# A two-block transformer kernel on one core: where the loads of the second feed forward's first two tiles stand in SyncE's queue

## The reference

```python
for l in range(DEPTH):                      # DEPTH = 2, h is 256 x 1024
    h = layer_norm(ALPHA * h + 0.5 * swiglu(h, ffn1_gate[l], ffn1_up[l], ffn1_down[l]), ...)
    ...                                     # token mixer, w_out, layer norm
    h = layer_norm(ALPHA * h + cross_attn(h, mem, ca_q[l], ca_k[l], ca_v[l], ca_o[l]), ...)
    h = layer_norm(ALPHA * h + 0.5 * swiglu(h, ffn2_gate[l], ffn2_up[l], ffn2_down[l]), ...)
# swiglu: (silu(x @ w_gate) * (x @ w_up)) @ w_down, inner width 2816 = 22 tiles of 128
# cross_attn ends with o @ ca_o, a 1024 x 1024 matrix
```

## Time and profile before

| | |
|---|---|
| median of three runs | 3466.71 us (3460.61 to 3467.05) |
| the profiled execution's own time | 3480.58 us |
| its span | 3478.8 us |
| mean granted TensorE clock | 0.985 of full speed |
| PE busy | 3171.2 us, 91% of the span |
| DVE busy | 2116.0 us, 61% |
| ScalarE busy | 936.6 us, 27% |
| GpSimd busy | 1198.1 us, 34% |
| bytes moved by DMA | 1163.11 MB, mean 334 GB/s |

### The profile page before, as it was taken

The page is one execution under the profiler, slowest core; times in us unless marked ns, Lnnn a source line. Parts: engine busy times, 40 slices in busy tenths (PEclk is TensorE's granted clock), DMA queues, the critical chain, the costliest instruction groups (busy, mean ns, idle before and its releaser), DMA issues.

```text
span 3478.8 us, 46441 instructions
## 1 busy us (share of the span) xinstructions
PE 3171.2 (91%) x16237; PEld 2519.7 (72%) x16237; DVE 2116.0 (61%) x4203; ACT 936.6 (27%) x2393; POOL 1198.1 (34%) x1129
## 2 busy tenths in 40 slices
PE   8899999989999999989999898878888889978887
PEld 5598888868878888868867655438877855636777
DVE  6686778655555458655554575676554477487544
ACT  2310022210010012220023354334443354433333
POOL 1003553334425433334410143344441044344332
PEclk9999999999999999999999999999999999999999
DMA  8578988689989977689963899999995399999998
GB/s 332 189 273 306 384 340 291 249 305 341 353 305 383 350 281 265 251 302 351 350 215 115 319 401 419 419 421 408 419 421 221 123 396 411 419 421 419 421 421 364
DMA packets 246943, 1163.11 MB, mean 334 GB/s; under 512 B 27256, under 2 KB 29656, under 8 KB 180720
## 3 DMA queue, kind: packets, MB, share of 16 engines
q0 software_dynamic: 152784, 825.30, 59.1%
q1 hardware_dynamic: 93936, 335.48, 27.1%
q10 hardware_dynamic: 48, 0.05, 0.0%
HBM read 1159.62 MB, written 1.10 MB: 334 GB/s over the span
## 4 chain that ended last, share of the span: by engine, by line
PE 60%; DMA 20%; DVE 6%; ACT 5%; issue 4%; POOL 1%; another core or an unknown queue 0%; SPq 0%; DVEq 0%; ACTq 0%; POOLq 0%
DMA ring<-in_peer_uv,idx 19%; PE ps_b L1040 17%; PE ps_a L1048 8%; PE ps_b L594 7%; PE ps_a L975 6%; PE ps_a L581 5%; PE ps_b L845 4%; PE ps_a L979 3%; ACT arena L1245 3%; PE ps_b L603 2%; DVE arena L2049 1%; ACT L1245 1%; ACT wts L1245 1%; DMA ring<-in_ffn 1%; PE ps_b L645 1%
## 5 line engine op out<-in xcount | busy, mean ns | idle before, releaser
L558 POOL DMA_INDIRECT ring<-in_peer_uv,idx x512 | 552.3, 1079 | 1144.3 <-PE ps_a L975 423.4
L2049 DVE SCALAR_TENSOR_TENSOR arena<-ring,h_tm 128x1024 f32<-128x1024 f32 x512 | 624.9, 1223 | 515.5 <-DMA ring<-in_peer_uv,idx 514.6
L520 POOL DMA_INDIRECT ring<-in_peer_uv,idx_now x512 | 574.1, 1121 | 407.4 <-DVE arena L1967 154.4
L1040 PE MATMUL ps_b<-x_t,ring 128*128 128x256 f32 x2816 | 622.2, 379 | 6.1 <-DMA ring<-in_ffn 3.2
L979 PE MATMUL ps_a<-arena,ring 128*128 128x128 f32 x4096 | 519.9, 283 | 107.8 <-ACT arena L1245 107.7
L1040 PEld LDWEIGHTS ps_b<-x_t,ring 128*128 128x128 f32 x2816 | 534.4, 190 | 81.5 <-DMA ring<-in_ffn 5.5
L979 PEld LDWEIGHTS ps_a<-arena,ring 128*128 128x128 f32 x4096 | 482.8, 195 | 145.9 <-ACT arena L1245 145.2
L975 PE MATMUL ps_a<-ring,arena 128*128 128x512 f32 x1024 | 485.2, 610 | 86.8 <-ACT arena L1245 85.7
L1245 ACT ACTIVATE arena<-ps_b 128x256 f32<-128x256 f32 (+2 forms) x213 | 104.0, 490 | 1324.3 <-PE ps_b L1040 771.2
L975 PEld LDWEIGHTS ps_a<-ring,arena 128*128 128x128 f32 x1024 | 182.2, 191 | 335.0 <-ACT arena L1245 175.6
L1048 PE MATMUL ps_a<-arena,ring 128*128 128x256 f32 x1408 | 318.7, 379 | 0.0
(11 more groups left out here) (273 smaller groups left out, 3201.1 us busy)
## 6 DMA issues: line engine op xcount, KB each, us to landing
ring<-in_ffn SPq DMA_DIRECT2D x264, 512.0 KB
wring<-in_second_w SPq DMA_DIRECT2D x232, 512.0 KB
wring<-in_mix_w SPq DMA_DIRECT2D x128, 512.0 KB
ring<-in_ada_rows POOLq DMA_DIRECT2D x36, 512.0 KB, 5.0
ring<-in_peer_uv,idx_now POOLq DMA_INDIRECT x512
ring<-in_peer_uv,idx POOLq DMA_INDIRECT x512
ring<-in_second_w SPq DMA_DIRECT2D x4, 512.0 KB, 15.4
ring<-in_c_rows POOLq DMA_DIRECT2D x1, 1024.0 KB, 7.3
```

The source lines that it names most:

```text
L520: G.indirect_dma_start(rows[:, s, :], None, table, bass.IndirectOffsetOnAxis(ap=idx_now[:, half, s:s + 1], axis=0)).then_inc(rows_in[s], p ...
L558: G.indirect_dma_start(pairs[:, slot, :, :].rearrange("p c d -> p (c d)"), None, a["peer_uv"], bass.IndirectOffsetOnAxis(ap=idx[:, b, s:s ...
L1040: ins = mm(bank[:, part * T:(part + 1) * T], fw[:, ft % 2, part, k * P:(k + 1) * P], x_t[:, k, :], start=k == 0, stop=k == KT - 1)
L2049: V.scalar_tensor_tensor(products[n % 2], pairs[:, at % PAIRS, 0, :], 1.0, h_tm[:, n // SLOTS, :], ALU.mult, ALU.mult, accum_out=dots[:, n ...
```

## The change

For the second feed forward (`w == 1`) of both layers, the call that loads the last four chunks of `mix_w` moves from behind the six loads of the first two tiles to ahead of them. Nothing else differs, and no other engine's program does.

```diff
                 for w in range(2):
+                    if w == 1:
+                        chunk_loads(a["mix_w"], mix_at + (MIX_CHUNKS - WR), WR)
                     for ft in range(2):
                         for part in range(3):
                             ff_loads(l * (2 * FT) + (w * FT + ft), ft, part)
                     if w == 0:
                         mod_row_loads(row_at)
                     else:
-                        chunk_loads(a["mix_w"], mix_at + (MIX_CHUNKS - WR), WR)
                         mod_row_loads(row_at + 1)
                         mod_row_loads(row_at + 2)
```

## The result

The changed kernel takes 3475.45 us (median of 19 runs, 3469.62 to 3484.81); the kernel before, beside it, 3466.02 us (19 runs, 3459.71 to 3471.03). The ratio is 1.0031, 95% interval 1.0023 to 1.0038: slower by 10.7 us (8.0 to 13.2); the medians alone are 9.4 us apart. I had forecast no change at 3466.7, with 3458 to 3474 as the range.

What follows compares the result with a forecast made beforehand. The prediction took PE, busy 3171.2 of 3478.8 us, to set the pace, with no load late on this stretch. All terms were 0, giving 3466.7 us from the runs' median, range 3458 to 3474.

Steps and rivals of the forecast that it cites:

- no change: Whole kernel: time stays at 3466.7 us, chance 0.75; about 0.2%, 7 us, taken as what a measurement can tell.
- What is taken away: Stretch from 709 to 727 us: 3.15 MB of loads leave it, the gathers and DVE don't move; gain 0.
- The output's second half: Its four chunk loads wait for PE's consumption at 746.27 and later, not for the six loads; gain 0.
- The six loads themselves: Issued from 756.85, landed by 767.2, first needed at 783.21: 16 us of cover; cost 0.
- No gathers are in the way: Six loads in their new place: POOL's last gather is issued at 745.04, so q1 runs at its own speed.
- The chunk behind the six: Modulation row's first chunk, queued behind the six: lands at 768.5, wanted at 770.18, 1.7 us to spare; cost 0.
- the second rival: Modulation row's first chunk lands after 770.18 and PE waits in each layer: up to +8.8 us, 3475.5 us; chance 0.12.
- The first rival: PE's idle time ahead of the output, behind ACT's late copy, goes with the loads: up to 10.8 us, 3456 us; chance 0.13.
- The sum against the profiled execution: Whole kernel: 0 against the profiled 3480.58 us, 13.9 us above the runs' median; change of 0 applied to 3466.71 us.
- A margin of 1.7 us: Modulation row's first chunk: time between its forecast landing and PE's need of it, in each layer.

Runs made afterwards that it cites:

- e8: Changed kernel with the modulation row's four chunk loads put ahead of the six loads, against the kernel before (3465.30 us chip): ratio 1.0007.
- e6: Changed kernel with MIX_SUMS 16, 16, 8 instead of 8, 16, 16 (fewer gathers in the stretch), against the kernel before: ratio 1.0041.
- e3: The change in the first layer only, against the kernel before (3491.43 us chip): ratio 0.9994.
- e10: Changed kernel with 16 matmuls of zeros ahead of the output's products in both layers, against the kernel before: ratio 1.0036.
- e2: Changed kernel with the modulation row's four chunk loads put ahead of the six loads, against the kernel before (3491.43 us chip): ratio 0.9988.
- e5: Kernel before with MIX_SUMS 16, 16, 8 instead of 8, 16, 16, old load order, against the kernel before: ratio 1.0052.
- e1: The kernel before again, no edit, against the kernel before (3491.43 us chip): ratio 0.9997.
- e12: The change in the first layer only, against the kernel before (3465.56 us chip): ratio 1.0018.

## Why the prediction was wrong

**What is taken away: right.** The 3.15 MB in the stretch to 727 us delayed nothing. e8 takes them away without the new wait and gains nothing.

**The output's second half: right.** L582 runs 27.89 us without a wait in the changed kernel.

**The six loads themselves: right.** The first gate product never waits for `ffn`, even in e8, where they go out 13.8 us later against the output's start than in the changed kernel.

**"No gathers are in the way": wrong, and this is the step that failed.** It rested on the time at which SP could issue: 756.85, worked out from the earlier trace rows. That time held PE's late start of the output (6.26 us) in it. POOL doesn't follow PE here, since DVE's sums, not the output, free its places. So when the stall (5.1 us) and the low clock behind it (2.1 us) are absent, and the values' products end 1.4 us earlier besides, SP's loads move up by 8.5 us and the gathers stay: last issue at 744.96 in the changed kernel, 745.04 in the earlier trace rows. An issue isn't a landing, either: in the trace of before, the queues from 746 to 750 us show

```profile
q0 software_dynamic: 421, 1.54, 99.4%
```

and 0.26 MB more from 750 to 754. At the forecast's 756.85 that was over. At 748.34 it wasn't: from 748 us on the changed kernel's gathers still move 1.6 MB, 1.6 MB / 0.41 = 3.9 us of all engines, in front of or between the six. They also hold up the four chunk loads ahead of the six, which by 748 us had moved only 1.04 of their 2.10 MB. The sum put right, an estimate with the forecast's own terms: 1.06 + 1.63 + 3.15 + 0.52 = 6.36 MB from 748.0 at 410 GB/s are 15.5 us, with its 1.8 us of latency 765.3; the profile has 765.89, and PE wants the chunk at 761.75. Without the 1.63 MB the same sum gives 761.3. That is just in time, as in e6. With PE late (e3, e10) there is room for the gathers.

**The chunk behind the six: right as a mechanism, wrong in its chance and its price.** This was the second rival, at 0.12 and +8.8 us. Its price came from an old burst's time per MB and was near by luck; the clock term of 1.4 us per layer wasn't in it. Nor do 7 us pass for no change here: with 19 runs a side the interval is 2.6 us to either side. The ring order that I cited from the Trainium skill, "DMA: Bandwidth & Descriptors", section "Queues, rings and completion order", is borne out: the chunk issued at 751.42 landed at 765.89, behind the six loads, the last of which landed at 764.61.

**The first rival: fell.** The late copy does go in the changed kernel's profile, as the rival said it would, but e2 and e3 have it with the loads moved, and e5 is without it with the loads in the old place. It goes with the chip: late in both layers of all three usable profiles where the kernel before takes 3491 us, in time in both layers of all eight experiments where it takes 3465 to 3466. The first profile of before is the one exception: it has the late copy (5.1 and 5.7 us), though the three plain runs beside it take 3461 to 3467 us, and on which chip it ran isn't known.

**The sum against the profiled execution.** I noted 13.9 us between that execution and the median and carried on. The stall ahead of the output and the low clock behind it are 5.1 + 2.1 us in the first layer and 5.6 + 3.0 in the second, 15.8 together: enough for the whole difference. The same holds on the chip of 3491 us: with these two terms taken out, the profiled executions of before, e1, e2 and e3 come to 3464.8, 3468.1, 3469.5 and 3467.3 us. The profile showed a case that the runs had not.

**What stays open.** Why the copy is late. It waits for `co_done`, which TensorE raises with its last product of the values. In the seven late places where the event is on record (both layers of the first profile, of e2 and of e3, the second of e1) it comes 5.1 to 11.0 us behind the products' modelled end, and the copy starts within 0.03 us of it. Whether the products really end late or only their signal does, no run here took apart. No packet of the instruction queues (q8, q14) starts between the products' end and the copy in any of the eight late places. That it depends on the gathers isn't shown either: e5 and e6 ran where it doesn't occur.

## What to carry to other kernels

When the profiled execution is slower than every plain run, find the rows that hold the difference before using its times, and take them out of every issue time and margin that follows from them. When a load is moved behind a wait, work out the landing of what stands behind it in the queue for the fastest case of the engine that it follows, with the traffic that doesn't follow that engine left where it is. A margin of 1.7 us next to an unexplained wait of 5 us is no margin.

## What the runs showed of the hardware

- A semaphore that TensorE raises with its last product came 5.1 to 11.0 us behind that product's modelled end in four profiles (before, e1, e2, e3), and within 0.02 us of it in both layers of the nine others (the changed kernel, e5 to e12); ScalarE's copy followed the signal within 0.03 us each time. The kernel before took 3491 us on the chip of e1 to e3 and 3465 to 3466 on the others.
- A wait of 4 us on TensorE cost 1.4 us more, since the next four matmuls ran at a lower granted clock (3.28 us for 1.88). Behind the longer stalls ahead of the output, 6.3 to 12.2 us, the products took 29.6 to 30.9 us for 27.89, 1.7 to 3.0 more, without growing with the stall. Behind waits of 3.69 and 3.20 us they took 3.20 and 2.74, behind 2.88, 1.73 and 1.07 us 1.88 each.
- SP's queue with a backlog and no gathers moved 4.05 MB from 756 to 766 us, 405 GB/s; with gathers beside it (748 to 756 us) each queue got about half, 1.69 and 1.60 MB.
